# One edit over the whole of a fused decoder-layer kernel: the opening loads, the softmax order, the router and the memory plan

## The reference

```python
h = rmsnorm(xp, norm_mix[l])
xr, q, k, v, g_rnn, g_attn = split_in(h, w_in[l])          # h @ w_in, 1024 x 4352
y_rnn, h_last = rg_lru(causal_conv(conv_in, ...), ...)     # a recurrence over positions
y_attn = window_attend(qb, kw, vw, qpos_p, kpos_p, attn_sinks[l])
xp = xp + merge_branches(y_rnn, y_attn, g_rnn, g_attn, w_out[l])   # sigmoid(g)*y, then @ w_out
xp = xp + moe(rmsnorm(xp, norm_ffn[l]), w_router[l], b_router[l], w_up[l], b_up[l], w_down[l], b_down[l])
# in moe:
logits = (t @ w_router + b_router)
top_v, top_i = lax.top_k(logits, 4);  wts = softmax(top_v)
z = xb @ w_up[e] + b_up[e]            # per expert e, the rows that chose it
y = x_glu * sigmoid(1.702 * x_glu) * (x_lin + 1.0)   # from z, clamped at 7
out += (y @ w_down[e] + b_down[e]) * weight
```

## Time and profile before

| | |
|---|---|
| median of 3 runs | 1142.85 us |
| the profiled execution's own time | 1141.49 us |
| its span, first to last instruction | 1139.7 us |
| TensorE busy | 1107.2 us, 97% of the span |
| VectorE, ScalarE, GpSimd busy | 27%, 20%, 3% |
| DMA, mean over the span | 384 GB/s, 437.90 MB in all |
| mean granted TensorE clock | 0.999 |
| chain that ended last | PE 69%, DMA 24%, DVE 3%, ACT 2%, issue 1% |

### The profile page before, as it was taken

One profiled execution on the slowest core, in us unless ns is written; L12 is line 12 of the kernel. 1 busy time (PEld: TensorE's weight loads), 2 busy tenths in 40 slices (PEclk: granted clock), 3 DMA queues, 4 the chain that ended last, 5 costly groups with the idle time before them and its releaser, 6 DMA issues.

```text
span 1139.7 us, 14908 instructions
## 1 busy us (share of the span) xinstructions
PE 1107.2 (97%) x5771; PEld 491.4 (43%) x5772; DVE 311.6 (27%) x790; ACT 228.7 (20%) x639; POOL 34.5 (3%) x71
## 2 busy tenths in 40 slices
PE   9999999999999999999999999999999999999997
PEld 6787878744343333333333333333232323232422
DVE  6565562122212121213031212121212120312123
ACT  3663544412020101010111111111111111010103
POOL 1200012200000000000000000000000000000000
PEclk9999999999999999999999999999999999999999
DMA  9843528999999999999999999999999999999995
GB/s 351 306 148 119 169 92 339 408 369 422 428 426 427 427 430 425 429 427 430 427 429 430 426 431 427 430 427 429 430 426 430 428 429 428 428 428 426 428 425 238
DMA packets 40651, 437.90 MB, mean 384 GB/s; under 512 B 6689, under 2 KB 9017, under 8 KB 10921
## 3 DMA queue, kind: packets, MB, share of 16 engines
q1 hardware_dynamic: 39984, 435.65, 91.7%
q10 hardware_dynamic: 624, 1.68, 0.4%
HBM read 436.00 MB, written 2.41 MB: 385 GB/s over the span
## 4 chain that ended last, share of the span: by engine, by line
PE 69%; DMA 24%; DVE 3%; ACT 2%; issue 1%; DVEq 0%; SPq 0%
PE bank L1339 22%; DMA ring<-in_w_down 20%; PE bank L1375 19%; PE bank L1074 8%; PE bank L1120 5%; PE bank L1221 4%; DMA area<-in_w_down 3%; PE bank L1242 3%; PE bank L1170 2%; PE bank L1255 1%; PE bank L1218 1%; PE bank L1245 1%; DVE area L1781 1%; PE bank L956 1%; PE bank L1056 1%
## 5 line engine op out<-in xcount | busy, mean ns | idle before, releaser
L1339 PE MATMUL bank<-ring,area 128*64 128x512 f32 x1744 | 396.4, 597 | 8.8 <-DMA ring<-in_w_up 8.6
L1339 PEld LDWEIGHTS bank<-ring,area 128*64 128x64 f32 x1744 | 117.1, 136 | 261.5 <-issue 225.3
L1375 PE MATMUL bank<-ring,area 128*64 128x512 f32 x928 | 213.8, 599 | 7.5 <-DMA ring<-in_w_down 7.5
L1769 DVE TENSOR_TENSOR x_tok<-x_tok,bank 128x512 f32<-128x512 f32 x60 | 41.3, 688 | 328.0 <-PE bank L1242 328.0
L824 ACT ACTIVATE area<-area 128x256 f32<-128x256 f32 x64 | 26.7, 417 | 515.7 <-DVE area L1781 515.7
L1074 PE MATMUL bank<-ring 128*128 128x264 f32 (+1 forms) x512 | 119.6, 391 | 0.0
L1375 PEld LDWEIGHTS bank<-ring,area 128*64 128x64 f32 x928 | 62.4, 136 | 117.9 <-issue 102.7
L1074 PEld LDWEIGHTS bank<-ring 128*128 128x128 f32 x512 | 95.8, 190 | 20.0 <-issue 1.3
L1806 DVE TENSOR_TENSOR area<-area 128x1024 f32<-128x1024 f32 x15 | 18.4, 1226 | 211.2 <-ACT area L834 211.2
L1242 PE MATMUL bank<-area 128*128 128x512 f32 x128 | 71.8, 644 | 0.0
L1339 PE MATMUL bank<-area 128*64 128x512 f32 x304 | 69.2, 597 | 1.1 <-DMA area<-in_w_up 1.1
(11 more groups left out here) (269 smaller groups left out, 693.5 us busy)
## 6 DMA issues: line engine op xcount, KB each, us to landing
ring<-in_w_up SPq DMA_DIRECT2D x103, 2048.0 KB, 33.4
ring<-in_w_down SPq DMA_DIRECT2D x51, 2048.0 KB, 33.1
area<-in_w_up SPq DMA_DIRECT2D x17, 2048.0 KB, 28.9
ring<-in_w_in SPq DMA_DIRECT2D x16, 1024.0 KB, 9.3
ring<-in_w_down SPq DMA_DIRECT2D x13, 1024.0 KB, 10.0
ring<-in_w_up SPq DMA_DIRECT2D x12, 1024.0 KB, 8.9
area<-in_w_down SPq DMA_DIRECT2D x5, 2048.0 KB, 33.4
ring<-in_w_out SPq DMA_DIRECT2D x8, 1024.0 KB, 5.0
```

The costliest lines, as they stand in the source:

```text
L1339: m = mm(bank[2 * h + n][64 * e:64 * e + 64, :], xe[:, k, 64 * e:64 * e + 64], w[:, kk, e, NB * n:NB * (n + 1)], start=False, stop=(k == K ...
L1375: m = mm(bank[4 + c][64 * e:64 * e + 64, :], y_t[:, 4 * half + f, 64 * e:64 * e + 64], w[:, f, e, :], start=False, stop=(half == 1 and f = ...
L1769: eng.tensor_tensor(x, x, combined_bank(unit, last)[:, :], ALU.add).then_inc(s.added, 1)
```

## The change

Four groups of edits.

**Memory plan.** The recurrence's factors `a_t` and `b_t` move to the start of the upper ring, so that slot 4 holds nothing else and is free after the recurrence; SP issues the first expert load (w_up, first pair, index 0) into it ahead of trunk load 16, after the recurrence. The loop of first loads then starts at 1, and its wait for `bias_step` goes. The expert biases are read into `h_tok` (which also is the key memory) after the sample rows' scores (`dsc_done`).

```diff
+        a_t, b_t = up(KB), up(KB)
...
-        pair_at = o
-        a_t, b_t, g_r, q_t = (up(KB) for _ in range(4))
+        open_at = o
+        g_r, q_t = up(KB), up(KB)
...
-        bias_in = upper[0:3 * E_N, pair_at:pair_at + 3 * D]
+        bias_in = h_tok[0:3 * E_N, :, :].rearrange("p a d -> p (a d)")
...
-            ends = (0, *(KB + k * (COLS + T) for k in (1, 2, 4, 6, KB)))
+            ends = (0, *(KB + k * (COLS + T) for k in (1, 2, 4, KB)))
...
+                elif n == 16:
+                    eng.wait_ge(s.lru_step, 2 * KB + 3)
+                    eng.dma_start(ring[:, RING // 2, :], w_up[0, 0]).then_inc(ring_full[RING // 2], 16)
...
-                    eng.wait_ge(s.lru_step, 2 * KB + 3)
+                    eng.wait_ge(s.dsc_done, 1)
...
             eng.wait_ge(s.attn_gated, KB)
-            eng.wait_ge(s.bias_step, 5)
...
-            for n in range(WIDE):
+            for n in range(1, WIDE):
```

```diff
-            eng.dma_start(keep[:, :], c_in[:, 0:C_KEEP]).then_inc(s.consts_loaded, 16)
...
             x_scale(5)
-            eng.wait_ge(s.open_loaded4, 16)
+            x_scale(7)
             act(sq[:, KB - 2:KB, :], x_raw[:, KB - 2:KB, :], ACT.Square).then_inc(s.sq_done, 1)
-            x_scale(7)
+            eng.dma_start(keep[:, :], c_in[:, 0:C_KEEP]).then_inc(s.consts_loaded, 16)
...
-            keep_warm(5, bank[7])
-            narrow_fills(16)
+            narrow_fills(36)
...
+                eng.wait_ge(s.consts_loaded, 16)
...
-                if k < 2 or k % 2 == 0:
-                    eng.wait_ge(open_loaded[k if k < 2 else k // 2 + 1], 16)
+                if k in (0, 1, 2, 4):
+                    eng.wait_ge(open_loaded[(0, 1, 2, 4).index(k)], 16)
                 eng.wait_ge(s.xn_a if k % 2 else s.xn_v, k // 2 + 1)
-                if k == KB - 1:
-                    norm_sum()
...
+                    if n == 2 and k == 3:
+                        norm_sum()
...
+            eng.wait_ge(s.sq_done, 1)
+            eng.tensor_tensor(sq[:, 0:2, :], sq[:, 0:2, :], sq[:, 2:4, :], ALU.add).then_inc(s.sq_add, 1)
             eng.wait_ge(s.open_loaded3, 16)
             v_scale(4)
+            v_scale(6)
             eng.tensor_tensor(sq[:, 4:6, :], x_raw[:, 4:6, :], x_raw[:, 4:6, :], ALU.mult).then_inc(s.sq_own, 1)
-            eng.wait_ge(s.sq_done, 1)
-            eng.tensor_tensor(sq[:, 0:2, :], sq[:, 0:2, :], sq[:, 2:4, :], ALU.add).then_inc(s.sq_add, 1)
-            eng.wait_ge(s.open_loaded4, 16)
-            v_scale(6)
```

```diff
-                if st >= 6 and st % 2 == 0 and st <= 2 * KB + 2:
-                    for jj in range((st - 6) // 2, (st - 4) // 2 if st < 2 * KB + 2 else KB):
-                        eng.wait_ge(s.pv_done, jj + 1)
-                        act(m_t[:, KB + jj, 0:2 * P], bank[5][:, 0:2 * P], ACT.Copy).then_inc(s.pv_evac, 1)
+                if st >= 6 and st % 2 == 0 and st <= 2 * KB + 2 or st == 2 * KB + 1:
+                    jj = (st - 6) // 2 if st <= 2 * KB else st - 2 * KB + 5
+                    eng.wait_ge(s.pv_done, jj + 1)
+                    act(m_t[:, KB + jj, 0:2 * P], bank[5][:, 0:2 * P], ACT.Copy).then_inc(s.pv_evac, 1)
...
+            def row_limit(j, p):
+                h = 2 * j + p
+                col = 16 * (j % 2) + 8 * p
+                eng.wait_ge(s.rowmax, 2 * h + 2)
+                eng.tensor_scalar(sm[:, col + 2:col + 4], sm[:, col + 2:col + 4], sinks[:, h:h + 1], -1.0,
+                                  ALU.max, ALU.mult).then_inc(s.negmax, 1)
...
                     eng.tensor_reduce(sm[:, col + 2:col + 3], buf[:, 0:P], AX.X, ALU.max).then_inc(s.rowmax, 1)
+                    if p:
+                        row_limit(j, 0)
                     eng.tensor_reduce(sm[:, col + 3:col + 4], buf[:, P:3 * P], AX.X, ALU.max).then_inc(s.rowmax, 1)
...
-                for p in range(2):
-                    buf, col = probs[:, 2 * (j % 2) + p, :], 16 * (j % 2) + 8 * p
+                    buf = probs[:, 2 * (j % 2) + p, :]
```

```diff
+            def logit_rows(t0, t1):
+
+                for t in range(t0, t1):
+                    n = P if t < 2 else TRIO
+                    eng.wait_ge(s.lt_ready, 1 if t < 2 else 2)
+                    own = lt[:, P * t:P * (t + 1)] if t < 2 else rs_tail[:, 0:TRIO]
+                    mm(lg_bank[t][0:n, :], own, stack, start=(t != 1), stop=False, skip_group_check=True)
+
+            def last_logits():
+
+                m = KB - 1
                 for t in range(3):
                     n = P if t < 2 else TRIO
-                    if t == 2:
-                        eng.wait_ge(s.lt_ready, 2)
-                    ml = mm(lg_bank[t][0:n, :], lt[:, P * t:P * t + n], stack, start=True, stop=True)
+                    eng.wait_ge(s.x2_ready, 3 * m + (2 if t == 2 else 1))
+                    own = x_res[:, m, P * t:P * (t + 1)] if t < 2 else xt[:, m % 2, 0:TRIO]
+                    ml = mm(lg_bank[t][0:n, :], own, wr[:, m, :], start=False, stop=True, skip_group_check=True)
                 ml.then_inc(s.logits_done, 1)
+
+            def last_sums():
+
+                eng.wait_ge(s.squares, SQUARES)
+                for t in range(3):
+                    n = P if t < 2 else TRIO
+                    m = mm(sum_cols[0:n, t:t + 1], last_sq[:, t, :] if t < 2 else tail_sq[:, 0:TRIO],
+                           ones_col, start=False, stop=(t == 2), skip_group_check=True)
+                m.then_inc(s.logits_done, 1)
...
-            keep_warm(2, bank[0])
+            logit_rows(0, 3)
+            eng.wait_ge(s.sumsq, 1)
+            mm(sum_cols, ident, stat[:, 0:3], start=True, stop=False, skip_group_check=True)
+            last_logits()
+            last_sums()
             token_rows(KB - 1)
-            logits(KB - 1, KB)
...
-            keep_warm(6, bank[0])
...
-            eng.wait_ge(s.split_copy, 6 * (KB - 1) + 2)
-            biases(0, 4, 0)
+            keep_warm(3, bank[0])
+            biases(0, 3, 0)
...
+            eng.wait_ge(s.split_copy, 6 * (KB - 1) + 2)
+            biases(3, 4, 3)
...
+            def first_tile(j, t):
+
+                if t == 0:
+                    eng.wait_ge(s.split_copy, 6 * j + 2)
+                r = slice(0, P) if t < 2 else slice(64 * (j // 4), 64 * (j // 4) + B_S)
+                rows = x_tok[r, t, P * j:P * (j + 1)] if t < 2 else x_tail[r, P * (j % 4):P * (j % 4 + 1)]
+                m = mm(first_bank(j)[:, P * (j % 4):P * (j % 4 + 1)], rows, gw[r, t, :], start=(t == 0), stop=(t == 2))
+                if t == 2:
+                    m.then_inc(s.gather_done, 1)
+
...
+                if j == 3:
+                    eng.wait_ge(s.flag_ready, 1)
+                for t in range(3):
+                    first_tile(j, t)
...
-                    keep_warm(4, bank[5])
-                    slot_rows(q, 5)
-                    first_rows(0)
-                    first_rows(1)
+                    for t in range(3):
+                        eng.wait_ge(s.oh_tile, t + 1)
+                        for j in range(2):
+                            first_tile(j, t)
...
+                ins = eng.scalar_tensor_tensor(out=lg[0:n, t, 0:E_N], in0=br[0:n, :], scalar=stat[0:n, 6 + t:7 + t],
+                                               in1=lg_bank[t][0:n, :], op0=ALU.mult, op1=ALU.add)
...
+            router_step(eng.scalar_tensor_tensor(out=rank_m[:, :, 0:2], in0=ranks[:, :, 0:2], scalar=1.0,
+                                                 in1=selb[:, :, 0:2], op0=ALU.add, op1=ALU.mult))
+            for t in range(3):
+                for e in range(2):
+                    ins = eng.scalar_tensor_tensor(out=gw[:, t, CAP * e:CAP * (e + 1)], in0=iota[:, 0:CAP],
+                                                   scalar=rank_m[:, t, e:e + 1],
+                                                   in1=stat[:, 9 + t:10 + t].to_broadcast([P, CAP]),
+                                                   op0=ALU.is_equal, op1=ALU.mult)
+                ins.then_inc(s.oh_tile, 1)
...
+                eng.tensor_scalar(xe[:, j, :], first_bank(j)[:, P * (j % 4):P * (j % 4 + 1)],
+                                  vec[:, NFF + j:NFF + j + 1], None, ALU.mult).then_inc(s.xt_ready, 1)
```

More of the change, by code:

```diff
@@ L781, in _ @@
                 tb, cols, half = bank[2 + m % 2], slice(P * m, P * (m + 1)), m // (KB // 2)
+                if m == KB - 1:
+                    eng.wait_ge(s.x2_ready, 3 * m + 1)
+                    act(last_sq, x_res[:, m, 0:2 * P].rearrange("p (t c) -> p t c", t=2), ACT.Square).then_inc(s.squares, 1)
+                    eng.wait_ge(s.logits_done, 4)
+                    act(stat[:, 6:9], sum_cols, ACT.Sqrt, bias=eps[:, :], scale=1.0 / D).then_inc(s.root, 1)
                 eng.wait_ge(s.h2_tr, m + 1)
-                for t in range(3):
+                for t in range(3) if m < KB - 1 else ():
                     n = P if t < 2 else TRIO
@@ L1715, in _ @@
[L1715 to L1724 removed]
+                if m < KB - 1:
```

(4 more changed lines are left out.)

135 lines of the change are left out of this document (61 added, 74 removed).

## The result

Over 8 runs each the changed kernel takes 1145.77 us (1144.54 to 1146.62) and the kernel before 1142.81 (1142.26 to 1143.52): ratio 1.0027, 95% interval 1.0018 to 1.0037, so 3.0 us slower (2.1 to 4.2). The forecast was +0.65 us, 1143.5; the measured time lies at the upper edge of its range (1145.8). The profiled execution took 1145.8, with a span of 1144.0 us, 4.3 more than before; the one before stood 1.3 us under its kernel's median, this one at its own, so the traces overstate the difference by about that much.

What follows compares the result with a forecast made beforehand. Expert weight transfers were taken to bound the kernel. The terms 2.4 - 0.8 - 0.4 - 0.85 + 0.3 gave +0.65 us, a forecast median of 1143.5 us, range 1140.8 to 1145.8.

Steps and rivals of the forecast that it cites:

- What bounds the kernel: Expert phase: paced by weight transfers at 429 GB/s; the end is R0 + 878.6 + 27.5 us.
- R0: Issue of the first expert load that waits for an expert matmul, 233.57 us in the kernel before.
- the same 878 to 879 us: Sign that the forecast is right: unchanged time from R0 to the last landing of a transfer.
- Memory plan: Expert loads: starting earlier only shifts the first ones, 12 are in place at R0 either way; 0 us.
- Opening: Kernel start: later norm_sum delays DVE's chain, so TensorE stands still ahead of the second gates; +2.4 us.
- Softmax: Attention, 80 to 165 us: two TensorE waits of 0.8 and 0.4 us go; -1.2 us.
- Router up to the first expert: From the output block's last add to the first expert matmul: shorter router steps; -0.85 us, range -0.4 to -1.4.
- Given back: Later six gathers, between expert matmuls: float32 costs +0.4 us for each of three pairs; +0.3 taken, bounds 0 and 1.2.
- Rival B: Ahead of the second gates: idle time drops TensorE's clock to 1.2 GHz; +3.9 us, 1147.4, chance 0.08.
- Rival A: Opening: its shift is hidden by unseen slack or an earlier landing; -1.75 us, 1141.1, chance 0.15.
- rival C: Expert loads: the memory plan puts one more load in place at R0; -4.25 us, 1138.6, chance 0.07.

Runs made afterwards that it cites:

- e13: Kernel before with only the change's opening, and 21 narrow fills to keep TensorE's loop at its place: 1144.74 us (1.0013 to 1.0032).
- e5: Changed kernel with the old order of the opening, but keeping the changed kernel's 36 narrow fills: 1143.84 us (1.0005 to 1.0023).
- e10: Changed kernel with norm_sum ahead of the first matmul of block n=2 instead of its fourth: 1144.97 us (1.0014 to 1.0032).
- e12: Kernel before with only the change's softmax edits: 1140.82 us (0.9980 to 0.9998).
- e14: Changed kernel with bf16 gathers for blocks 2 to 7 of the first pair, four more useless wide matmuls, 17 narrow fills: 1143.17 us (1.0001 to 1.0019).
- e8: Kernel before with three useless 1.07 us float32 matmuls behind the pairs of later gathers, six narrow fills fewer: 1144.25 us (1.0007 to 1.0025).
- e3: Changed kernel with the old opening and bf16 gathers for blocks 2 to 7 of the first pair: 1140.74 us (0.9979 to 0.9997).
- e11: Changed kernel with the first expert load issued again behind the trunk instead of inside it: 1146.45 us (1.0020 to 1.0044), 6 runs.
- e6: e3 with four more useless wide matmuls in the router and four narrow fills fewer: 1140.75 us (0.9977 to 0.9995).
- e7: Changed kernel with 22 instead of 36 narrow fills at its start: 1152.46 us (1.0072 to 1.0100).
- e15: Kernel before with 10 instead of 16 narrow fills, its loop ending at instruction 5553: 1148.64 us (1.0043 to 1.0070).

## Why the prediction was wrong, point by point

- What bounds the kernel: right that transfers pace the end, wrong in taking the time behind R0 as fixed. I had named "the same 878 to 879 us" from R0 to the last landing as a sign. R0 hardly moved (233.62 for 233.57), but that stretch grew to 882.8 us.
- Memory plan, 0: right. The early loads put the changed kernel 6.3 MB ahead at 200 us, but between 200 and 220 us it moves 181 GB/s instead of 429, since the remaining loads wait for their slots, and at R0 the two are level at 56.9 MB.
- Opening, +2.4: right in mechanism and size: 2.5 us at the gates, 2.4 alone (e13), 1.5 to 1.9 given back (e5). Moving norm_sum forward brings the gates 1.0 us earlier (e10), though its median doesn't show it.
- Softmax, -1.2: right, -1.5 alone (e12).
- Router up to the first expert, -0.85: right, -0.84 in the trace.
- **"Given back", +0.3 with bounds 0 and 1.2: this is the step that failed.** It has two errors. The price per pass, 0.11 us, was taken from L1164, whose passes stream 32 columns; the gather streams 128, and its passes take 0.16 on the token rows and 0.2 on the 8 sample rows, 1.05 us a block instead of 0.65. So three pairs cost 3.7 us, not 1.2. And I let only a quarter of it count, since R0 stands ahead of it. But behind R0 each group of loads waits for the next group of matmuls while the DMA engines are not yet full: 3.4 us of transfer are lost between 235 and 290. e14 takes 2.1 us back, and e8, a plain delay at the same place, shows that 1.8 of 3.2 us, nearly 60%, arrive in the median.
- With +3.4 in that place the sum is 2.4 - 0.8 - 0.4 - 0.85 + 3.4 = +3.75; by e8's share, 3.7 us would count 2.1 and the sum would be +2.45. Measured were +3.0 (2.1 to 4.2), between the two. Which of them is nearer is open.
- Rival B named a real mechanism at the wrong place. At the second gates the clock stayed 1.00. In the router, where the change leaves fewer useless matmuls, it falls in the profiled executions of e3, e10 and e11, and the first 16 expert matmuls then take 5.3 us (e11: 6.5) instead of 3.65. The changed kernel's profiled execution, which stands at its median, has 1.00 there, so its 3.0 us don't need it; that it fell in some of the others is not excluded. Rival A fell with e5 and e13, rival C with e11.

The best kernels here are e3, e6 and e12: 1.7, 1.7 and 1.5 us under the kernel before (the intervals end at 0.03%, 0.05% and 0.02% under it). e12 has the softmax alone, so of the router's and the memory plan's edits nothing measurable is left on top of it.

## What to carry to other kernels

Price a matmul by a row with the same number of streamed columns and rows of contraction, not by one of the same dtype. Where the transfers become the bound only after a ramp, count TensorE's work inside the ramp in bytes not moved; being level at its start says nothing. And when two kernels with a loop differ in length, look for waits without a releaser at the turns of the loop, and compare the packets of the instruction queues, before believing any difference of a few us.

## What the runs showed of the hardware that I had not expected

- The turn of TensorE's loop of some 1,750 instructions costs nothing with its branch at instruction 5565, 5567 or 5569, and 3 to 7.5 us of waits at each of three turns at 5539, 5541, 5553, 5597, 5629 and 5655. In total that is 6 to 7 us of a kernel's time (e7, e15). The waits go with fetches of instructions: 54 or 55 packets of 16 KB on the instruction queue instead of 28. Why the place decides whether the loop is fetched again is open; no run here shows a rule for it.
- TensorE's clock went to its lower level (1.2 GHz, windows of 0.50) at 230 to 234 us (e3, e10; to 236 in e11) behind stretches where TensorE was busy 1.4 to 1.7 of 2 us. The changed kernel's profiled execution had the same (1.65, 1.46 and 1.69 of 2 us from 226 to 232) and stayed at 1.00, and e3's mean clock was 0.997 in three executions and higher in eight. The Trainium skill, "TensorE: Matmul & The Clock Gate" (Part 1: The HAM clock gate), says that the moment at which the clock rises varies from run to run. No run here shows that moment; the executions of e3 differ in the same way in whether the clock falls.
